# A gate matrix made by adding transfers instead of one-hot products, in a transformer layer with retrieved experts

## What is computed

```python
def peer_block(hb, w_q, keys, u, v):
    """sum_h sum_{e in top-k(h)} softmax(score)_e * v_e * gelu(u_e . x)."""
    q = (hb @ w_q).reshape(T, 8, 2, 128)                  # 8 heads
    s = einsum('thpd,pkd->thpk', q, keys)                 # 2 x 128 sub-keys
    top_s, top_i = top_k(s, 16)
    cand_s = top_s[:, :, 0, :, None] + top_s[:, :, 1, None, :]
    cand_i = top_i[:, :, 0, :, None] * 128 + top_i[:, :, 1, None, :]
    best_s, pos = top_k(cand_s, 16)                       # 16 of 16,384 experts per head
    idx, g = cand_i at pos, softmax(best_s)
    act = gelu(einsum('thkd,td->thk', u[idx], hb))
    return einsum('thk,thkd->td', g * act, v[idx])
```

## Time and profile before

| | us |
|---|---|
| runs (3): lowest, median, highest | 3524.42, 3536.6, 3547.55 |
| the profiled execution | 3525.8 |
| its span, from the first to the last instruction | 3524.0 |
| its mean granted TensorE clock | 0.95 of full speed |

### The profile page before, as it was taken

The page is one execution under the profiler, slowest core; times in us unless marked ns, Lnnn a source line. Parts: engine busy times, 40 slices in busy tenths (PEclk is TensorE's granted clock), DMA queues, the critical chain, the costliest instruction groups (busy, mean ns, idle before and its releaser), DMA issues. The chain is left out here.

```text
span 3524.0 us, 44194 instructions
## 1 busy us (share of the span) xinstructions
PE 3244.8 (92%) x15044; PEld 2588.0 (73%) x15044; DVE 2414.0 (69%) x3842; ACT 1023.1 (29%) x1185; POOL 1889.4 (54%) x1401
## 2 busy tenths in 40 slices
PE   8999589996999998999899799999999999999997
PEld 4689465574888887787787577777777777777776
DVE  3111465443588887787667578888878888887878
ACT  2110134422333323444344222222222222222221
POOL 1000224403333324566566677777777778777874
PEclk9999678997999999999999899999999999999999
DMA  9110000022322323444544689988898988898887
GB/s 350 48 54 32 10 13 25 6 99 106 100 98 92 104 80 112 143 156 142 189 146 146 230 287 293 298 284 295 282 291 290 297 291 286 282 296 288 277 282 278
DMA packets 327176, 649.93 MB, mean 184 GB/s; under 512 B 168736, under 2 KB 170032, under 8 KB 324016
## 3 DMA queue, kind: packets, MB, share of 16 engines
q1 hardware_dynamic: 234544, 342.28, 30.3%
q0 software_dynamic: 91392, 272.96, 22.6%
q10 hardware_dynamic: 1152, 33.55, 2.3%
HBM read 573.18 MB, written 75.50 MB: 184 GB/s over the span
## 5 line engine op out<-in xcount | busy, mean ns | idle before, releaser
L2025 DVE SCALAR_TENSOR_TENSOR total<-ex_ring,ex_pick,total 128x1024 f32<-128x1024 f32 x512 | 649.6, 1288 | 262.0 <-DMA ex_ring<-peer_v_dram,sp_row 256.7
L1882 POOL DMA_INDIRECT ex_pick<-act_scratch,sp_place x512 | 596.5, 1165 | 173.9 <-issue 155.8
L1887 POOL DMA_INDIRECT ex_ring<-peer_v_dram,sp_row x512 | 599.6, 1171 | 156.0 <-issue 143.8
L1915 PE MATMUL ex_dots<-h_hi_b,ex_uhi 128*128 128x512 f32 x1024 | 399.7, 390 | 13.7 <-ACT ex_uhi L1957 13.7
L1915 PE MATMUL ex_dots<-h_lo_b,ex_uhi 128*128 128x512 f32 x1024 | 399.6, 390 | 0.0
L1976 ACT ACTIVATE ex_whi<-ex_act 128x512 fp32r<-128x512 f32 x128 | 81.1, 633 | 960.6 <-DVE ex_act L2004 960.6
L1273 POOL TENSOR_TENSOR ga_ulo<-ga_u,ga_uhi 128x1024 fp32r<-128x1024 f32 x72 | 181.5, 2522 | 219.6 <-ACT ga_uhi L1267 211.1
L1761 DVE TENSOR_TENSOR gm_b_lo<-gm_iota,second_T 128x1024 fp32r<-128x1024 f32 x64 | 189.8, 2965 | 145.5 <-PE gm_prod L1703 144.7
L1925 PE MATMUL ex_y<-ex_vhi,ex_whi 128*128 128x512 f32 x512 | 218.2, 426 | 68.5 <-DVE total L1994 62.9
L1918 PE MATMUL ex_dots<-h_hi_b,ex_ulo 128*128 128x512 f32 x1024 | 254.6, 391 | 6.6 <-DVE ex_ulo L1986 6.6
L1273 POOL TENSOR_TENSOR ra_ulo<-ra_u,ra_uhi 128x1024 fp32r<-128x1024 f32 x56 | 141.1, 2521 | 217.6 <-ACT ra_uhi L1267 217.6
(11 more groups left out here) (287 smaller groups left out, 7365.9 us busy)
## 6 DMA issues: line engine op xcount, KB each, us to landing
ex_u<-peer_u_dram SPq DMA_DIRECT2D x128, 512.0 KB, 4.6
ex_v<-peer_v_dram SPq DMA_DIRECT2D x128, 512.0 KB, 7.6
ga_u<-peer_u_dram SPq DMA_DIRECT2D x72, 512.0 KB, 3.6
gate_scratch<-gm_out ACTq DMA_DIRECT2D x8, 4096.0 KB, 11.8
ex_g<-gate_scratch SPq DMA_DIRECT2D x128, 256.0 KB, 6.1
ra_u<-peer_u_dram SPq DMA_DIRECT2D x56, 512.0 KB, 3.6
w_ada_half<-w_ada_dram SPq DMA_DIRECT2D x12, 2048.0 KB, 14.6
act_scratch<-ga_act SPq DMA_DIRECT2D x72, 256.0 KB, 2.2
```

The source lines that it names most:

```text
L1882: nc.gpsimd.indirect_dma_start(weights[:, i:i + 1], None, places, bass.IndirectOffsetOnAxis(ap=picks[:, i:i + 1], axis=0)).then_inc(pick_i ...
L1887: nc.gpsimd.indirect_dma_start(ring[:, i], None, rows, bass.IndirectOffsetOnAxis(ap=which[:, RING * s + i:RING * s + i + 1], axis=0)).then ...
L1915: nc.tensor.matmul(dots[:, c], uhi[:, c, kk], b[:, kk], start=kk == 0 and b is hi, stop=False)
L2025: nc.vector.scalar_tensor_tensor(total[:, t], ring[:, i], weights[:, bass.ds(PER * s + i, 1)], total[:, t], ALU.mult, ALU.add).then_inc(ro ...
```

## The change

The gate matrix lies in HBM as [second key j, first key i, token of half B] (128 x 128 x 512 floats, 32 MB). It is cleared in `gated_linear` by 16 transfers from a tile of zeros, with SP waiting for them within that block. In `route` GpSimd then issues, for each head, each of its 16 picks and each of the 4 tiles of half B, one indirect transfer that adds 128 gates (one per token) at their places: 8 x 16 x 4 = 512. Two heads can pick the same expert for a token, so the transfers of a head wait until all of the head before have landed.

The stage `gate_matrix` is gone. All 128 chunks of half A are made in `route`: six per head, 80 behind the heads. GpSimd makes the low halves of the first 62 (`POOL_LOWS`) and DVE those of the other 66. The adding transfers are spread: none in heads 0 and 1, five behind each low half in heads 2 to 7 (180), two behind each of the 14 low halves that follow (28), the other 304 in a row. DVE calculates the place of every pick in each head, so that the picks need no turning. The exponents of the last head stand before chunk 60 on ACT.

In `experts` the gates of a chunk are one contiguous piece of 256 KB, loaded as 128 rows of 2 KB; the picks lie in another order, with the same number of gathers.

```diff
+CLEARS = 16
@@ gated_linear, SP
+                sp.wait_ge(nothing_ready, 1)
+                for n in range(CLEARS):
+                    at = slice(n * KEYS // CLEARS, (n + 1) * KEYS // CLEARS)
+                    sp.dma_start(gates[at].rearrange("j i t -> i j t"),
+                                 nothing[:].unsqueeze(1).to_broadcast([P, KEYS // CLEARS, TBD])).then_inc(gates_clear, 16)
+                sp.wait_ge(gates_clear, 16 * CLEARS)
@@ gated_linear, GpSimd
+                nc.gpsimd.memset(nothing[:], 0.0).then_inc(nothing_ready, 1)
@@
-PER_STEP = 18
-STEPS = 4
-AFTER_HEADS = 8
-ROUTED = PH * PER_HEAD + AFTER_HEADS
-assert ROUTED + STEPS * PER_STEP == KEYS
+IN_HEADS = PH * PER_HEAD
+ROUTED = KEYS
+POOL_LOWS = IN_HEADS + 14
+EXP_AT = IN_HEADS + 12
+SPREAD = 5
@@ route, SP
+                for b in range(2):
+                    sp.wait_ge(scattered[b], 16 * PER_SPOT * PH // 2)
@@ route, GpSimd
+                def scatter(n):
+                    h, q, t = n // PER_SPOT, n % PER_SPOT // NB_TILES, n % NB_TILES
+                    if n % PER_SPOT == 0:
+                        pool.wait_ge(place_ready, h + 1)
+                        pool.wait_ge(gate_ready, h + 1)
+                        if h:
+                            pool.wait_ge(scattered[1 - h % 2], 16 * PER_SPOT * ((h + 1) // 2))
+                    at = h * TOPK + q
+                    nc.gpsimd.indirect_dma_start(
+                        spots, bass.IndirectOffsetOnAxis(ap=place[:, NA + t, at:at + 1], axis=0),
+                        gate[:, NA + t, at:at + 1], None, compute_op=ALU.add).then_inc(scattered[h % 2], 16)
...
+                spots_done = 0
+                for h in range(PH):
+                    for c in range(PER_HEAD):
+                        ahead.split_low(pool, PER_HEAD * h + c, c % 2, h == 0 and c < 2)
+                        if c % 2 and c < 4 and h < PH - 1:
+                            split(h + 1, c // 2)
+                        for _ in range(SPREAD if h >= 2 else 0):
+                            scatter(spots_done)
+                            spots_done += 1
+                for n in range(IN_HEADS, POOL_LOWS):
                     ahead.split_low(pool, n, n % 2, False)
+                    for _ in range(2):
+                        scatter(spots_done)
+                        spots_done += 1
+                for n in range(spots_done, PER_SPOT * PH):
+                    scatter(n)
@@ route, TensorE: the turning of the picks is gone
+                with pe.Fori(IN_HEADS // 2, ROUTED // 2) as pair:
+                    for c in range(2):
+                        ahead.dots(pe, 2 * pair + c, c, False)
@@ route, DVE, at the end of a head
+                    link(nc.vector.scalar_tensor_tensor(expert[:, :, here], second_key[:], float(KEYS), first_key[:],
+                                                        ALU.mult, ALU.add))
+                    nc.vector.scalar_tensor_tensor(place[:, :, here], expert[:, :, here], float(TBD),
+                                                   sparse.token[:].unsqueeze(2).to_broadcast([P, NT, TOPK]),
+                                                   ALU.mult, ALU.add).then_inc(place_ready, 1)
@@ route, DVE, behind the heads
+                dve.wait_ge(ahead.ulo_ready, POOL_LOWS)
+                with dve.Fori(POOL_LOWS // 2, ROUTED // 2) as pair:
+                    for c in range(2):
+                        ahead.split_low(nc.vector, 2 * pair + c, c, False)
@@ gate_matrix: the whole stage is gone
-def gate_matrix(nc, d, hi, lo, first_T, second_T, gate_T, scratch, acts):
...
@@ experts, SP
-                    sp.dma_start(g[:, c].rearrange("p (b t) -> p b t", b=NB), src).then_inc(g_in[c], 16)
+                    sp.dma_start(g[:, c], one(scratch, n, "a i t -> (a i) t")).then_inc(g_in[c], 16)
@@ trunk
-    gates = nc.dram_tensor("gate_scratch", [NB, P, KEYS, TB], F32)
+    gates = nc.dram_tensor("gate_scratch", [KEYS, P, TBD], F32)
```

267 lines of the change are left out of this document (60 added, 207 removed).

## The result

The changed kernel takes 3701.2 us (median of 4 runs, 3690.2 to 3713.0) against 3532.5 us for the kernel before on the same chip (3524.4 to 3547.6): a ratio of 1.047, interval 1.042 to 1.052. It was forecast at 3387, in a range that ended at 3515. The forecast is wrong in its sign, by 314 us. Some executions of a kernel come out over 1.5% above its fastest one; medians and ratios here leave those out.

What follows compares the result with a forecast made beforehand. TensorE was taken to bound routing, GpSimd's issuing the expert stage. After the change GpSimd ends the routing stage: -150.9 + 1 = -149.9 us gives a run of 3376, plus 11 a median of 3387; range 3335 to 3515.

Steps and rivals of the forecast that it cites:

- The price of an adding transfer: On GpSimd in routing: 1.35 us in the heads, 1.27 behind them, mean 1.30, 664.6 us for 512 transfers.
- The adding rival: On GpSimd: adding costs a third descriptor per element, 1.72 us a transfer, 215 us more, 3602 in total; chance 0.20.
- VectorE beside the transfers: In the heads: full blocking of GpSimd behind wide DVE products would add 82 us; 0.1 of the forecast's chance.
- The rest of the sum on GpSimd: From 989.7 to 1822.4 without idling: besides transfers, low halves 123.4, query splits 25.1, changes of head 19.6; together 832.7 us.
- Changes of head: On GpSimd: 7 waits until a head's last transfer has landed, 2.8 us each, 19.6 us.
- TensorE in the heads: GpSimd's round of 60.6 us against a head's 59.57; TensorE loses 15 us, covered by GpSimd's later end.
- TensorE behind the heads: 5.60 us a chunk, TensorE ending at 1799, 27 us before GpSimd's last transfer; no slowing by transfers counted.
- the rival in which transfers hide behind TensorE: Transfers at 1.25 us and free changes of head end at 1778, before TensorE's 1784; total 3348, chance 0.09.
- The clearing: Behind the constants: 33.55 MB at 375 GB/s take 89.5 us, almost hidden within its block; counted as 1 us.
- The rival of half the rate: The clearing outlasts its block at half the DMA rate: 84 us more, 3471 in total; chance 0.07.
- The expert stage: Lasts 1510 us as before, with the same 1024 transfers at 1.46 us; 0 gain counted from larger gate loads.
- break-even of 1.59: On GpSimd: price in us per adding transfer from which the adding rival decides, 1.30 + 150 / 512.

Runs made afterwards that it cites:

- e1_plain: The changed kernel with its 512 transfers writing plainly instead of adding, part of the output left out: 3887.1 us, kernel before on that chip 3665.2.
- e2_gather: The changed kernel with its 512 transfers gathering the same gate matrix places into an SBUF tile, dense half's output left out: 3857.8 us.
- e3_add_sbuf: The changed kernel with its 512 transfers gathering the gate matrix places with an addition into a cleared SBUF tile, dense half's output left out: 3844.4 us.

## Why cheap transfers alone don't bring the gain either

With plain writes the forecast's sum holds on GpSimd and fails on TensorE. TensorE's timeline in e1_plain (start, duration, idle before):

```profile
1515.02 0.39 PE L1293 MATMUL ra_dots<-h_lo_a,ra_uhi 128*128 128x512 f32 x1 [0.46 <-issue]
1517.12 0.40 PE L1293 MATMUL ra_dots<-h_hi_a,ra_uhi 128*128 128x512 f32 x1 [1.71 <-issue]
1519.90 0.59 PE L1293 MATMUL ra_dots<-h_lo_a,ra_uhi 128*128 128x512 f32 x1 [2.39 <-issue]
1522.01 0.59 PE L1293 MATMUL ra_dots<-h_hi_a,ra_uhi 128*128 128x512 f32 x1 [1.51 <-issue]
```

VectorE's:

```profile
1510.34 1.22 DVE L1283 TENSOR_TENSOR ra_ulo<-ra_u,ra_uhi 128x1024 fp32r<-128x1024 f32 x1 [42.26 <-issue]
1575.39 1.23 DVE L1283 TENSOR_TENSOR ra_ulo<-ra_u,ra_uhi 128x1024 fp32r<-128x1024 f32 x1 [63.83 <-issue]
```

and ScalarE's:

```profile
1641.08 1.28 ACT L1305 ACT_TABLE_LOAD   x1 [65.72 <-remote]
```

One matmul in 2 to 3 us, each behind a wait named issue; one chunk in some 65 us in place of 5.6. ScalarE waits up to 65.7 us before a table load, by a releaser named remote: a semaphore event that no instruction in the profile accounts for. The windows of e1_plain, before and in this stretch:

```profile
1341.00:1440.00 99.00, 99.00 (x434) 79.75 (x433) 58.55 (x221) 34.83 (x43) 87.51 (x60) 1.00 0.40 136
...
1500.00:1700.00 200.00, 38.15 (x72) 20.85 (x72) 3.67 (x3) 7.19 (x8) 148.03 (x154) 0.53 0.05 12
```

The DMA engines are busy for 0.05 of the time, so it isn't their bandwidth. The stretch begins some 40 us behind GpSimd's last low half (1429.3), from which on its transfers follow each other without a break at 0.96 + 0.30 = 1.26 us (the distance at the median; the mean from 1500 to 1700 is 1.31), and ends some 20 us behind the last transfer. Distances below are medians too. I call it the stall; the expectations say that TensorE crawls. R is the theory that the rate of the transfers does it, L that the loops do, H that the chip does. The gather of e2_gather shows it too (38.8 of 200 us), e3_add_sbuf with its 1.84 us a transfer doesn't (199.5 of 200).

> The kernel with plain writes once more, because in its first run the transfers took 0.96 us each but TensorE issued one matmul every 2.8 us while GpSimd issued them without a pause, on a chip on which the kernel before took 3665 us too. If the rate of the transfers does it by itself (R), TensorE crawls here too, from about 1450 until the last transfer, and the kernel is slower than the one before. If it is that chip (H), then on a chip where the kernel before takes 3530 the route stage ends near 1825 and the total is near 3390.

The same kernel on the second chip: 3928.7 us, ratio to before 1.052, interval 1.039 to 1.066. TensorE is busy for 181.6 of the 459 us from 1341 to 1800, where the first chip had 194.6.

These two chips also run the kernel before more slowly than the 3532 of the result. Its profile on one of them:

> The kernel before, unchanged, profiled on the chip of this call, so that the kernels of this call have a trace of before beside them. Theory R (TensorE, VectorE and ScalarE get their instructions late while GpSimd sends indirect transfers without a break): what differs from the first chip lies in the expert stage alone, where GpSimd issues the large gathers, as waits named issue or remote; border near 1977. Theory H (another chip is slower all over): the gate stage is longer too.

Measured: 3705.1 us. The expert stage starts at 1968.1 there, no later than the earlier trace rows; it lasts 1735 us instead of 1547. All that this chip loses is in the expert stage. The waits of the kernel before, first on this chip, then in the profile that the prediction read:

```profile
ACT ex_act L1972 <- remote: 419.1, 34, 24.9
```

```profile
ACT ex_whi L1976 <- DVE ex_act L2004: 960.6, 128, 10.3
```

(us in total, times, longest.) These are the longest sums of the two profiles. On this chip it is ScalarE's wait by the releaser named remote, the one that the stall has; on the first chip the kernel before has no such wait at all. Nor have the changed kernel there and the three whole kernels below, on another chip with the kernel before at 3530; all other profiles of this document, taken on the slower chips, have it. So the expert stage of this chip looks like a mild form of the stall: its GpSimd too does nothing but indirect transfers. That is a likeness in the rows, not shown to be one cause: the gathers of this stage follow each other at 1.25 us at the median on either chip, and on the first one TensorE works through them.

**Without loops.** Each engine's chunk loop behind the heads was written out (`with pe.Fori(...)` became `for pair in range(...)`, on ScalarE, VectorE and SyncE too), still with plain writes.

> Leaves out the adding: 512 plain indirect writes, so picks of one token that name one expert are not summed. Beside it the chunk loops behind the heads are written out on TensorE, ScalarE, VectorE and SyncE, 39 or 40 pairs without a loop. Theory L (at the end of a loop's body each engine refetches its instructions, and that fetch is what comes late): TensorE is busy over 400 of the 459 us from 1341 to 1800, border near 1915. Theory R (the transfers delay every instruction fetch, loop or not): TensorE is busy under 250 of the 459 us, as with the loops (195 and 176), last chunk near 2168.

Measured: 3779.4 us, before there 3711.2. TensorE 210.0 of the 459 us, 42.7 of 200 between 1500 and 1700. The loop's jump isn't it: L falls.

**Paced.** Behind the transfers stands a memset, wide, then narrower, then none:

```diff
                 for n in range(spots_done, PER_SPOT * PH):
                     scatter(n)
+                    wide = 512 if n < 308 else 256 if n < 408 else 0
+                    if wide:
+                        if n > spots_done:
+                            pool.wait_ge(padded, n - spots_done)
+                        nc.gpsimd.memset(pad[:, 0:wide], 0.0).then_inc(padded, 1)
```

> Leaves out the adding as well. Of the 304 transfers behind GpSimd's last low half, the first 100 have a 512-column memset behind each (about 0.5 us, so one transfer in 1.85 us, the pace of the adding ones), the next 100 one of 256 columns (about 0.3 us, 1.6 us a transfer), the last 104 none (1.26 us). If the rate decides (R), TensorE stays busy at 1.85 us a transfer, from about 1404 to 1590; between 1590 and 1750 the threshold shows itself; behind 1750 it crawls at one matmul in about 2.8 us until the last transfer near 1880. If the kind of transfer decides (plain ones stall the others, adding ones don't), it crawls from about 1450 whatever the pace.

Measured: 3589.9 us where before takes 3711.2, one run each. GpSimd's timeline where the 256-column memsets end:

```profile
1779.52 0.97 POOL L1415 DMA_INDIRECT gate_scratch<-sp_gate,sp_place  x1 [0.16 <-issue]
1780.48 0.33 POOL L1443 MEMSET ro_pad<- 128x256 f32 x1
1780.97 0.96 POOL L1415 DMA_INDIRECT gate_scratch<-sp_gate,sp_place  x1 [0.16 <-issue]
1782.24 0.95 POOL L1415 DMA_INDIRECT gate_scratch<-sp_gate,sp_place  x1 [0.30 <-issue]
```

and the windows (same columns):

```profile
1600.00:1700.00 100.00, 100.00 (x430) 80.62 (x429) 22.06 (x18) 40.18 (x45) 88.46 (x123) 1.00 0.43 140
1700.00:1800.00 100.00, 100.00 (x430) 80.58 (x429) 20.89 (x17) 38.64 (x43) 85.87 (x114) 1.00 0.43 138
1800.00:1850.00 50.00, 8.72 (x37) 6.41 (x35) 1.23 (x1) 2.73 (x4) 36.76 (x39) 0.64 0.06 16
```

At 1.67 and at 1.46 us a transfer TensorE is full, 459.0 of 459 us up to 1800, on a chip where it stalled at 1.26. From 1800 on it is idle for another reason: its last dot product ends at 1809.8, and nothing is left to do. That the stall comes back behind the last memset (1780.5) shows on ScalarE, whose last GELU starts at 1827.24, after 15.67 us of waiting:

```profile
1827.24 0.60 ACT L1305 ACTIVATE ra_act<-ra_dots 128x512 f32<-128x512 f32 x1 [15.67 <-remote]
```

These transfers don't add, and they don't stall the others; so it isn't adding that spares TensorE in the changed kernel, and this run speaks for how close the transfers come.

**Whole kernels with plain writes.** A plain write may stand in for an adding one if the sum is made before. In the next kernels VectorE compares the experts of each head with those of every earlier head and adds the gates of equal picks; heads are written in order, so the last write of a place holds the whole sum. Nothing is left out. A memset stands behind each of the last 304 transfers, in the first two kernels only up to number 470. For a pair of heads (cut):

```diff
+                    summing(nc.vector.tensor_tensor(same[:], expert[:, NA:, now].unsqueeze(3).to_broadcast(wide),
+                                                    expert[:, NA:, then].unsqueeze(2).to_broadcast(wide), ALU.is_equal))
+                    summing(nc.vector.tensor_tensor(same[:], same[:],
+                                                    gate[:, NA:, then].unsqueeze(2).to_broadcast(wide), ALU.mult))
+                    summing(nc.vector.tensor_reduce(part[:], same[:], AX.X, ALU.add))
+                    before = gate[:, NA:, now] if g == 0 else whole[:, :, now]
+                    last = nc.vector.tensor_tensor(whole[:, :, now], before, part[:], ALU.add)
```

> A whole kernel, nothing left out: 512 plain indirect writes, the sums made beforehand. VectorE adds to each gate of head h, for every earlier head, the gates of picks that name the same expert (28 pairs of heads, 4 operations each, estimated at 3.9 us a pair: 6 pairs inside heads 2 to 4, 22 pairs between its low halves behind the heads); heads are written in order, so the last write of a place holds the whole sum. Behind GpSimd's last low half a 256-column memset stands behind each transfer up to number 470, as in the run before, where that gave one transfer in 1.46 us with TensorE at work. Price theory (0.96 us a plain transfer, and the stream's rate decides on TensorE): last transfer between 1855 and 1900, first large gather right behind, total some 90 us below the kernel before on the same chip, ratio 0.970 to 0.980. If the 28 pairs lengthen the heads on VectorE by more than the 23 us of their work, TensorE finishes its chunks behind 1860 and the ratio is 0.98 to 1.0.

> As g1_totals, with memsets of 128 columns (estimated 0.2 us, of which 0.14 lies in the 0.30 us between transfers that are there anyway: one transfer in about 1.32 us). If the rate decides and its threshold lies between 1.32 and 1.46 us, TensorE crawls again from about 1460, its last chunk lies behind 1950 and the ratio is above 0.99. If an instruction of another kind between two transfers is what lets the others in, whatever its length, TensorE stays busy to about 1810 and the last transfer lies near 1820 to 1840: ratio 0.955 to 0.97.

> As g2_totals_128, with memsets of 8 columns and one behind each of the 304 last transfers. A memset of one column took 0.10 to 0.12 us in the kernel before, and behind a memset the gap before the next transfer was 0.16 instead of 0.30 us, so the transfers come 0.96 + 0.16 + 0.11 = 1.23 us apart: closer than the 1.26 us of the plain row at which TensorE all but stopped. If the rate decides, TensorE crawls from about 1460 and the ratio to the kernel before is above 1.0. If what counts is that an instruction of another kind stands between two transfers, TensorE stays busy to about 1810, the last transfer lies near 1404 + 304 x 1.26 (with the longer transfers that a refill brings) + 10 = 1797 to 1830, and the ratio is 0.955 to 0.965.

| kernel | memset, columns | distance of transfers | experts start | us | ratio to before, interval |
|---|---|---|---|---|---|
| g1_totals | 256 | 1.46 us | 1922.3 | 3476.6 | 0.985, 0.981 to 0.988 |
| g2_totals_128 | 128 | 1.35 us | 1873.1 | 3430.3 | 0.973, 0.969 to 0.977 |
| g3_totals_8 | 8 | 1.27 us | 1866.2 | 3429.9 | 0.974, 0.970 to 0.978 |

All three ran on a chip where the kernel before takes 3526 to 3530 us. All three came out above what was expected of them (0.970 to 0.980, 0.955 to 0.970, 0.955 to 0.965), as their last transfers start at 1915.1, 1865.8 and 1858.9, later than counted. What wasn't counted are longer transfers: in g1_totals the mean is 1.11 us where the median is 0.965. Here too they stand beside VectorE, which has the sums to make: 83 of the 334 that overlap one of its instructions are long, and none of the 178 that overlap none. By the mean, g2_totals_128 and g3_totals_8 send a transfer in 1.42 and 1.40 us behind the low halves, which is why they take the same time. The window of g3_totals_8 and its timeline:

```profile
1500.00:1700.00 200.00, 200.00 (x859) 161.15 (x858) 106.70 (x103) 79.42 (x90) 166.74 (x278) 1.00 0.43 141
```

```profile
1467.40 0.96 POOL L1420 DMA_INDIRECT gate_scratch<-ro_whole,sp_place  x1 [0.19 <-issue]
1468.36 0.12 POOL L1447 MEMSET ro_pad<- 128x8 f32 x1
1468.67 0.96 POOL L1420 DMA_INDIRECT gate_scratch<-ro_whole,sp_place  x1 [0.18 <-issue]
```

1.27 us apart and TensorE is full. That looked as if a memset between two transfers were enough, whatever the distance (a short break in place of the rate). But the stalled rows had run on other chips. So both were measured on one chip, with plain writes and no sums; h3_plain_wait has a wait in place of the memset. The edit of h2_plain_memset8 behind the plain writes:

```diff
                     scatter(n)
+                    if n > spots_done:
+                        pool.wait_ge(padded, n - spots_done)
+                    nc.gpsimd.memset(pad[:, 0:8], 0.0).then_inc(padded, 1)
```

> The same kernel as e1_plain (leaves out the adding), as the base of this call: the two runs with a short memset between the transfers stood on another chip than the unbroken rows, so what they differ in may be the chip. If the unbroken row is what stops TensorE, it does so here too, with under 250 of the 459 us from 1341 to 1800 busy, wherever this call runs. If it is a property of the two chips seen so far, TensorE may be busy for over 430 here on a chip where the kernel before takes about 3530.

> Leaves out the adding. Differs from h1_plain_third in one thing: behind each of the last 304 transfers stand a wait that is always met and a memset of 8 columns (0.12 us), which leaves the distance of the transfers at 1.27 us. Theory B (the unbroken row): TensorE busy over 430 of the 459 us from 1341 to 1800, chunks done near 1805, last transfer near 1858. Theory R (the rate): as h1_plain_third, whatever stands between.

> Leaves out the adding. As h1_plain_third with only a wait between the last 304 transfers, always met, and no memset. If the semaphore wait is what breaks the row, TensorE is busy for over 430 of the 459 us; if it takes an instruction that computes, or the extra time, it is under 250 as with the unbroken row.

| kernel (before there 3674.1) | us | TensorE busy of 459 us (1341 to 1800) |
|---|---|---|
| h1_plain_third, unbroken | 3839.8 | 199.8 |
| h2_plain_memset8 | 3825.8 | 261.2 |
| h3_plain_wait, a wait alone | 3822.9 | 188.0 |

The theory of the break falls. On this third of the slower chips the short memset at 1.27 us lets little through, 84.5 of 200 us from 1500 to 1700 against 43.4 without it, and the wait does nothing. The rows speak for the distance, and for a limit that depends on the chip: 1.46 us is free on a chip that stalls at 1.26; 1.27 stalls on one chip and is free on another, the one where the kernel before is at 3530. GpSimd sends equally many transfers in those 200 us on both, 141 here and 139 in g3_totals_8. That kernel has the sums besides, but they aren't what keeps TensorE going, as the next kernel shows.

> As g3_totals_8 without the memsets: the last 304 transfers in an unbroken row, 1.26 us apart, sums made by VectorE, nothing left out. Where the kernel before takes over 3660 on the chip of the call, both theories expect TensorE all but stopped (under 250 of the 459 us from 1341 to 1800) and a ratio above 1.03. Where it takes about 3530: if the stall belongs to the chips on which the kernel before is slow too, TensorE is busy for over 430 of the 459 us, the last transfer lies near 1838 and the ratio is 0.965 to 0.975; if the unbroken row does it on every chip, TensorE is under 250 and the ratio above 1.03.

This is g3_totals_8 without its memsets, so with an unbroken row. It ran on a fourth chip, again of the slower kind: 3732.6 us, before there 3683.4, ratio 1.014, interval 1.008 to 1.021. In its profiled execution, a longer one of 3758.0 us, TensorE was busy for 334.1 of the 459 us, and for 126.1 of the 200 from 1500 to 1700, sums and all. Here the stall brakes itself: GpSimd waits 131.3 us for VectorE's sums, and in those waits the others get on. So it stays open whether an unbroken row at 1.26 us stalls a chip where before takes 3530, and through what the stall acts. DMA bandwidth is excluded by its share (0.05), the loops by f1_plain_no_loops. That instructions or tables reach the other engines late fits the names issue and remote; it is argued from the names alone. The DMA queue named instruction speaks neither for nor against more fetching: from 1500 to 1830 it moved 2 packets in e1_plain and 2 in the changed kernel, which doesn't stall.

## Why the prediction was wrong, point by point

- **The price of an adding transfer: the step that failed.** The prediction took 1.35 and 1.27 us from the gather of single elements, with ends at 1.25 and 1.46. It is 1.94: 1.641 busy and 0.302 of issue. On the sum: 995.1 us in place of 664.6, 330.5 more. The adding rival had a price of 1.72, a chance of 0.20 and a time of 3602. Its sign was right, its size two thirds of what was missing (215 of 330.5 us): it scaled the median of 0.947 us by descriptors alone, which gives 1.42 where 1.555 was measured, and left out the 0.086 us of the longer transfers. By the two sizes the greater part of the surplus is a charge per transfer, not one per element. For its ground it cited the Trainium skill (Collectives: The Full Stack, section The bandwidth ceiling), that an add emits two read descriptors where a copy emits one. The traces agree that the addition has its price in issuing wherever the destination lies; the records show 144 packets where a plain transfer has 32, not a count of descriptors.
- **The bound excluded the unknown.** No row of before showed an operation that adds, and both ends of the forecast's range were rows of operations that don't. Its argument against the rival, gathers of 4 KB and of 4 B at one price, says nothing of an addition.
- **VectorE beside the transfers: below its worst case.** The prediction set 82 us for full blocking behind the wide products, with a chance of 0.1. The longer transfers sum to 44.0 us above the median (512 x 0.086). The 26 that overlap the product of picks and keys (`ro_pick`, L1625) are all long, so VectorE does hold some back, but it explains 44 of the 330.5 us.
- **The rest of the sum on GpSimd: right.** From 986.4 (989.7 forecast) to 2144.1 are 1157.7 us; forecast 832.7; the difference is 325.0, and the transfers make 330.5 of it. Changes of head and waits for TensorE cost 14.1 + 6.5 us where 19.6 stood for the changes of head. The low halves show a mean of 2.97 us in this stretch, but their spans overlap those of the transfers: the groups of this stretch sum to 840.3 + 145.5 + 29.5 = 1015.3 us (transfers, low halves, splits), GpSimd's busy time in the windows from 977 to 2155 to 986.8. Less the overlap, low halves and splits took 146.5 us, forecast 148.5. With plain writes the last transfer starts at 1833.1, its end forecast at 1822.4.
- **TensorE in the heads: wrong with the price.** Two query splits one head apart start at 1104.24 and 1183.87, so a head takes 79.6 us where 59.6 and at most 62 were forecast. GpSimd's round is 8 x 2.4 + 30 x 1.94 = 77.4 us. The form of the step was right: the longer round of the two sets the head.
- **TensorE behind the heads: right, by luck.** From 1500 to 1900 it is full, at the old 5.6 us a chunk, and then idles for 245 us where 25 were forecast. But the prediction took for granted that transfers don't disturb TensorE. At the price that it forecast they do, on all four of the slower chips; the rival in which transfers hide behind TensorE would have failed there too.
- **The clearing: right.** The block behind it starts at 471.17 (SyncE's timeline), 2.2 us before the 473.32 of the earlier trace rows; +1 was forecast. In the window from 378 to 473 the DMA engines move 364 GB/s at a share of 0.99. The Trainium skill (DMA: Bandwidth & Descriptors, section Latency and other measured facts) has 207 GB/s for a pitch of 512 KiB from one partition's row to the next. In this clearing the rows of neighbouring partitions lie 2 KB apart, and only the eight pieces of one partition step by 256 KiB. So the prediction held the figure against a layout that it isn't for, and the measurement doesn't test it. The rival of half the rate is out.
- **The expert stage: right.** 3697.9 - 2149.2 = 1548.7 us against 3524.0 - 1977.3 = 1546.8. The gate load lands in 5.2 us in place of 6.1, and VectorE's wait for rows is 260.2 against 256.7: shorter loads gave nothing.
- **Chances.** Faster had 0.80. The case that came was the one in which the operation that no row showed was dear, and its 0.20 was cut to 0.15 by a price too near the break-even of 1.59.

## What to carry to other kernels

An operation that only looks like a measured one is unmeasured: an indirect transfer that adds takes 1.55 us of GpSimd where a plain one takes 0.96. If the order of the writes is known, make the sums before and write plainly; with a short memset behind each transfer that turned a loss of 4.7% into a gain of 2.6% here. And where GpSimd sends hundreds of small transfers close together, look at every other engine for waits named issue or remote, on more than one chip. The gain of 2.6% was measured on one chip, and with the transfers 1.46 us apart the plain writes were the faster ones on a slower chip too (3589.9 against 3711.2, one run, without the sums). At 1.27 us they weren't.

## What the runs showed of the hardware

- The surplus of adding is 0.60 us for 128 elements and 0.53 for 64, to HBM as to SBUF.
- 128 single elements of 4 B cost GpSimd the same written as gathered: 958 and 944 ns.
- Indirect transfers of single elements in an unbroken row, 1.26 us apart, nearly stop TensorE, VectorE and ScalarE on three chips (TensorE 37 to 43 of 200 us), with the DMA engines at a share of 0.05 to 0.07; on a fourth they halt them in part (126 of 200). At 1.46 us, on one of the three, they don't. No chip with the kernel before at 3530 ran such a row.
- In the expert stage of the kernel before, gathers take longer only beside VectorE: of the 932 that overlap one of its instructions 392 take over a tenth more than the median, and of the 92 that overlap none not one does.
- An 8-column memset between two transfers takes 0.12 us, and the gap of issue falls from 0.30 to 0.18, so the distance at the median grows by 0.01 us only; the last of 304 transfers still came 26.5 us later (1858.3 in h2_plain_memset8 against 1831.8 in h1_plain_third).
- Chips differ by up to 6% on the same kernel (3530 to 3731 us); where one of the slower ones was profiled, the whole difference lay in the expert stage (1735 against 1547 us).
